# A written order for the interleaved steps of two hybrid blocks, in place of a greedy planner

## What is computed

```
out_a = sliding_window_attention(rope(norm(aq)), rope(norm(ak)), av, sinks)      # 8 heads, window 128
out_b = rmsnorm(hgrn2(bq, log_f(bf), bv)) * silu(bg)                             # 4 heads, decayed linear attention
out_c = rmsnorm(gated_delta(silu(conv4(cqkv)), beta, g)) * silu(cg)              # 4 heads, a triangular inverse per chunk
```

## Time and profile before

| what | value |
| --- | --- |
| runs | 4287.96, 4295.01, 4295.93 us; median 4295.01 |
| profiled execution, its span from the first to the last instruction | 4287.7 us (its own time outside the span is not shown) |
| PE / PE weight load / DVE / ACT / POOL busy | 93 / 76 / 60 / 38 / 3 % |
| instructions on PE / DVE / ACT | 20700 / 4066 / 2881 |
| mean granted TensorE clock | 0.955 of 2.4 GHz |
| the chain that ended last | PE 80 %, DVE 12 %, ACT 5 % |

### The profile page before, as it was taken

One profiled execution on the slowest core, in us unless ns is written; L12 is line 12 of the kernel. 1 busy time (PEld: TensorE's weight loads), 2 busy tenths in 40 slices (PEclk: granted clock), 3 DMA queues, 4 the chain that ended last, 5 costly groups with the idle time before them and its releaser, 6 DMA issues.

```text
span 4287.7 us, 51835 instructions
## 1 busy us (share of the span) xinstructions
PE 3992.2 (93%) x20700; PEld 3250.2 (76%) x20700; DVE 2571.8 (60%) x4066; ACT 1621.0 (38%) x2881; POOL 108.0 (3%) x199
## 2 busy tenths in 40 slices
PE   5879999998889999999999999999899999999988
PEld 5759778877768788887777677767777777777776
DVE  6767365654576432456667743776566667546765
ACT  3343232243443332333444243553334343334532
POOL 0000000000000000000000000000000000000000
PEclk9979799998899799989999999999899999999999
DMA  6502155532111232333232223233232322221233
GB/s 219 171 5 89 50 168 196 188 118 65 60 40 69 72 101 84 106 100 104 91 99 72 74 89 94 64 104 126 80 119 85 108 70 84 84 88 56 84 113 113
DMA packets 216641, 417.93 MB, mean 97 GB/s; under 512 B 16384, under 2 KB 61472, under 8 KB 214608
## 3 DMA queue, kind: packets, MB, share of 16 engines
q1 hardware_dynamic: 197584, 335.12, 24.4%
q0 software_dynamic: 18816, 79.49, 5.4%
HBM read 378.89 MB, written 35.67 MB: 97 GB/s over the span
## 4 chain that ended last, share of the span: by engine, by line
PE 80%; DVE 12%; ACT 5%; issue 2%; DMA 1%; SPq 0%; DVEq 0%; ACTq 0%; POOLq 0%
PE ps L632 59%; PE ps L104 13%; DVE arena L126 3%; PE ps L115 3%; ACT arena L200 3%; DVE arena L141 2%; DVE spl L126 2%; PE ps L2292 2%; DVE X L126 1%; DVE HF L126 1%; DVE sm L147 1%; PE ps L2287 1%; ACT sph L200 1%; PE ps L882 1%; PE ps L110 1%
## 5 line engine op out<-in xcount | busy, mean ns | idle before, releaser
L126 DVE TENSOR_TENSOR spl<-ring,sph 128x1024 fp32r<-128x1024 f32 (+2 forms) x556 | 651.5, 1178 | 731.9 <-ACT sph L200 730.7
L200 ACT ACTIVATE sph<-ring 128x1024 fp32r<-128x1024 f32 (+2 forms) x556 | 562.4, 1023 | 776.6 <-PE ps L632 758.3
L632 PE MATMUL ps<-sph,HTh 128*128 128x512 f32 (+3 forms) x1680 | 668.9, 398 | 22.6 <-DVE HTl L126 11.7
L632 PE MATMUL ps<-spl,HTh 128*128 128x512 f32 (+3 forms) x1680 | 621.5, 370 | 0.0
L632 PE MATMUL ps<-sph,HTl 128*128 128x512 f32 (+3 forms) x1680 | 620.6, 369 | 0.0
L200 ACT ACTIVATE arena<-ps 128x512 f32<-128x512 f32 (+2 forms) x570 | 314.0, 563 | 727.8 <-PE ps L632 484.3
L632 PE MATMUL ps<-HTh,sph 128*128 128x512 f32 x1360 | 540.5, 397 | 17.1 <-DVE spl L126 14.9
L632 PE MATMUL ps<-HTl,sph 128*128 128x512 f32 x1360 | 532.5, 392 | 0.0
L632 PE MATMUL ps<-HTh,spl 128*128 128x512 f32 x1360 | 532.1, 391 | 0.0
L104 PE MATMUL ps<-arena 128*128 128x128 f32 (+6 forms) x2264 | 374.0, 349 | 52.3 <-ACT arena L200 29.9
L632 PE MATMUL ps<-sph 128*128 128x512 f32 x992 | 405.6, 409 | 7.4 <-DVE spl L126 7.4
(11 more groups left out here) (219 smaller groups left out, 5105.3 us busy)
## 6 DMA issues: line engine op xcount, KB each, us to landing
ring<-in_w_in SPq DMA_DIRECT2D x264, 512.0 KB, 3.6
arena<-in_ada_w SPq DMA_DIRECT2D x88, 512.0 KB, 4.7
ring<-in_w_down SPq DMA_DIRECT2D x44, 512.0 KB, 3.3
ring<-in_w_gate SPq DMA_DIRECT2D x40, 512.0 KB, 3.8
ring<-in_w_up SPq DMA_DIRECT2D x40, 512.0 KB, 3.8
ring<-in_w_mem SPq DMA_DIRECT2D x32, 512.0 KB, 3.3
ring<-in_w_out SPq DMA_DIRECT2D x32, 512.0 KB, 3.9
ring<-in_w_br_ssd SPq DMA_DIRECT2D x32, 512.0 KB, 3.9
```

What stands on the lines that cost most here:

```text
L126: self.e.tensor_tensor(o, a, b, op).then_inc(*self.done.up())
L200: self.e.activation(o, a, f, **kw).then_inc(*self.done.up())
L632: ins = pe.e.matmul(o, l, r, start=k0 == 0 and i == 0 and not b.pairs, stop=k0 + b.ks == b.kt and i == 3 * b.ks - 1 and (c0 > 0 or not b.p ...
```

## The change

The planner, its constants, the lists of start slots and gates and `slot_after` are gone. For the stages `ada0`, `mix 0`, `mix 1`, `proj 0` and `proj 1` the order is written down as a string: one letter per step, `M` for main, a number before a letter repeats it. `steps_of` reads it; all engines follow it. The two `ffn` stages have main alone. The number of steps of each stream is the same as before, the generators and their waits are not touched, and SP's list of weight loads does not depend on the order. `ada0`'s string is the order that the planner made; the other four differ from the planner's throughout.

```diff
-SLACK = 1.5
-STEPS = 3
...
+STREAMS = {
+    "mix": dict(M="main", c="conv", g="gdn", a="att", h="hgrn", i="inv", m="mem", b="back", t="angles"),
+    "proj": dict(M="main", c="conv0", d="conv1", s="ssd", p="pass", g="gated", t="turns", f="diff", n="dnorm", x="cross0", y="cross1", z="cross_t", m="mgt", r="rest"),
...
+SCORES = {
...
+    ("mix", 0):
+        "14Mt2Mt2Mt6Mt4MtM2a9M2a4Mh7Mch2MaMc8MaMh8Ma4MaMac2Ma3Ma3Ma2Mc3MacMat3MaMh2MhM2c5Ma2c6gagaghaha2gagha"
+        "g2agagag2agagagag3agag3a4gimh2imhim4MiM2ihiMh2MiMihiMh2MiMhMiMiMhiMh2Mi2M3ihiMhihi2h3MiMh2MihMih2ihi"
+        "hih3i2M2h5M2iM2i3M2i25Mb",
+    ("mix", 1):
+        "26M2a3MaMa3MahMhMcMcMaMc2aMaM2aMaMcMac2Ma6M2aMhMa7Mahc6Mc2MaMacMac2h6M2gh5gah2gaga2ga2gag2a2g2ag2aga"
+        "g2agaga2gagihmimimh3MihMi3MihMiMih2MiMhiMiMhiMiMhMihi2MiMhMihiMihiM2ih2MhMiMhM2ihihMihiMh3ihi2M2hi4M"
+        "iMi3M3i10Mb15M",
+    ("proj", 0):
+        "35McMdMd3Md8Md3M2d2Md2Mc4McMdc2Mcdc7M5c2M2dMcMsMcd2Mc5MscMdM2dMcdMdMc3Md6M2cMsdc2MdsMc4Mc2dcd2Mc2M2c"
...
+        "2Mpsp2Msp2sp2sMpMpMs2pMpsM2p2Mp2M2p2MpM2pM3p2MpM3pg2M3pMp2M2pMg3MpM2p2M3pMpM3p2M2p2Mp2Mpg3pM3p19Mg4M"
+        "g6MgMg3Mgt3Mt5Mt3M2t2Mt2Mt2Mtgt8Mt2Mt3MtM4tMt4M2t5M2t2M2t15Mt7MtMt5Mt7Mt10MtM2t15M2tg3MfM2f2Mf2Mf4Mf"
...
+        "2n3MyMy6Mx3Mz3MzM2z6Mz24MmMm15Mm3M2m27M",
+    ("proj", 1):
+        "17Ms3MrMr2M2r7Msd6Md7MdMc6Mc3MdcMcMc2McMdcd2McMd5Md2MdM2cd3M2cd6Md3MdMcd2M2dcMcdMd2c5Md2McMc3Mc2d2sM"
...
+def steps_of(phase):
+    names, n = STREAMS[phase[0]], ""
+    for ch in SCORES[phase]:
+        if ch.isdigit():
+            n += ch
+            continue
+        for _ in range(int(n or 1)):
+            yield names[ch]
+        n = ""
...
-        def weave(q, phase, main, sides, gates=(), chain=(), turn=1 << 30):
+        def weave(q, phase, main, sides=()):
+
+            gens = dict(sides)
             gens["main"] = main
+            if phase in SCORES:
+                for name in steps_of(phase):
                     next(gens[name], None)
...
-            starts = [("conv", (), {0: conv[1], **conv}), ("gdn", ("conv",), slot_after(name, ("hvb", l, 1))),
-                      ("att", (), slot_after(name, ("kvb", l))),
-                      ("hgrn", (), {0: slot_after(name, ("hzb", l, 1)), 8: ("att", 99), 22: slot_after(name, ("hvb", l, 1))}),
...
-            return {slot_after(k, ("hvb", l, 1)): [("mem", 99)], w: [("hgrn", 99)], w + 8: [("inv", 99)]}
...
-            weave(q, k, main(q, k), second_sides(q, l) + [("rest", rest, (), 0)] * l, second_gates(l))
+            weave(q, k, main(q, k), second_sides(q, l) + [("rest", rest)] * l)
```

More of the change, by code:

```diff
@@ L386, in take @@
             return banks[i]
-        def weave(q, phase, main, sides, gates=(), chain=(), turn=1 << 30):
-            gens = {name: gen for name, gen, _, _ in sides}
+        def weave(q, phase, main, sides=()):
+            gens = dict(sides)
             gens["main"] = main
-            if phase in plans:
-                for name in plans[phase]:
+            if phase in SCORES:
+                for name in steps_of(phase):
                     next(gens[name], None)
[L398 to L456, removed]
-                for name, n in gates.get(slot, ()):
-                    while name not in over and count.get(name, 0) < n:
-                        go_on()
-                step("main")
-                slot += 1
-                for _ in range(STEPS):
-                    who = pick([(d, n) for d, n in can() if d <= q.t + SLACK])
-                    if who is None:
-                        break
-                    step(who)
-            slot = 1 << 30
-            while len(over) < len(gens):
-                go_on()
-            plans[phase] = plan
@@ L472, in program @@
+            for name, gen in gens.items():
+                for _ in gen:
+                    assert name == "main" and phase not in SCORES, (phase, name, q.name)
         groups, order, then, turned = {}, [], {}, {}
@@ L1876, in mixers @@
                      act=(conv1_act, gdn_act, att_act, hgrn_act, inv_act, mem_act, idle))
[L1877 to L1883 removed]
+            names = ("conv", "gdn", "att", "hgrn", "inv", "mem", "back")
             fs = f.get(q.name, [idle] * 7 if q.name == "sp" else [idle] * 5 + [mem_pool, back_pool])
[L1885 removed]
+            out = [(n, g(q, l)) for n, g in zip(names, fs)]
             if l == 0:
                 g = dict(pe=angles_pe, dve=angles_dve, act=angles_act).get(q.name, idle)
[L1888 removed]
+                out.append(("angles", g(q, l)))
             return out
@@ L2023, in first @@
                 ht_begin(q, k, xn, [(k, "xn", m) for m in (0, 1, 2, "half", 3)])
-            weave(q, k, main(q, k), mixers(q, l), mix_gates(l), CHAIN, slot_after(k, ("hvb", l, 1)))
+            weave(q, k, main(q, k), mixers(q, l))
             k = ("ffn", l)
@@ L2039, in first @@
                     layer_in(q, 0)
-            weave(q, k, main(q, k), [])
+            weave(q, k, main(q, k))
         XS = ar(0, 4, 4, 512)
@@ L2929, in second_sides @@
-            ssd[unit(12)] = [("conv0", 99), ("conv1", 99)]
-            half = pass_steps(16)
-            passes = {0: [("conv0", 99), ("conv1", 99), ("ssd", unit(18))], half: ("ssd", unit(34))}
-            gated = {0: s("z", l, 0), 2: s("z", l, 1), 4: s("z", l, 2), 6: s("z", l, 3)}
-            turns = {2 * n: s(("dq", "dk")[n // 4 % 2], l, n // 8) - 3 + n % 4 for n in range(16)}
-            turns[0] = [turns[0], ("gated", 8)]
-            b1 = slot_after(k, (("br", l, 0), 1))
-            empty = iter(())
```

89 lines of the change are left out of this document (28 added, 61 removed).

## The result

The kernel with the written order takes 4099.68 us (median of 4 runs, 4095.03 to 4101.13), the kernel before 4295.03 us (4287.96 to 4295.93). The ratio is 0.9552, 95 % interval 0.9538 to 0.9566: 4.5 % faster. The forecast was 4217 us in a range from 4155 to 4285; the sign and most of the places were right, the size was not: 195 us were saved where 78 were expected.

What follows compares the result with a forecast made beforehand. PE, busy 93 % of the span, was taken as the bound, losing time to waits and half clock in stages with side steps. Terms -25 - 12 - 6 - 50 + 15 = -78 from 4287.7, plus 7.3, gave 4217 us; range 4155 to 4285.

Steps and rivals of the forecast that it cites:

- lead-in: Mixers, between last projection slot and `gdn`: most of the dry stretch goes, moved PE work paid beside main; 25 us saved.
- `gdn` to first memory slot: Mixers: `hgrn` steps enter in layer 0, three `inv` steps leave in layer 1 and are paid after; 0 net.
- chain over the states: Mixers, after the first memory slot: main slots kept for the chain reduce half clock; 6 us saved per layer, 12.
- `hgrn`'s first step: `mix 1`: placed one slot later, so the next chunk's splits come before ACT is taken; 6 us of a 12.85 us wait saved.
- second block: `proj 0` and `proj 1`: half of 91 us of PE waits go, 46, and 4 for the end parts' clock; 50 us saved.
- new waits: Clusters of side steps and more side work beside the mixers' projection stand in front of splits; 15 us added.
- the slower rival: Clusters of side steps on DVE stand in front of splits PE needs, making them late; 4320 us, chance 0.08.
- More is saved: State chains keep full clock and second-block waits nearly all go; -140 us, 4155 us, chance 0.22.
- The clock oscillates: In the second block a finer weave would make PE's clock fall over a third of 2400 us; 4310 us, chance 0.04.

Runs made afterwards that it cites:

- head_new: Written order to the last projection slot in the mixers and to slot 208 in the second block, then the planner's order of the kernel before: 4205.5 us.
- to_memory: Written order to the first memory slot in the mixers and to slot 464 in the second block, then the planner's order of the kernel before: 4153.4 us.
- hgrn_later: The written-order kernel with the first two `hgrn` steps of `mix 1` three main slots later: 4105.34 us.

## Why the prediction was right or wrong

The terms of the sum, each with what the trace after shows:

| term | forecast | measured |
|---|---|---|
| lead-in, net of the work moved | -25 | -48.8 |
| `gdn` to first memory slot | 0 | -31.0 |
| after it (chain over the states) | -12 | -11.1 |
| `hgrn`'s first step | -6 | -2.4, within the first term |
| second block, waits and clock | -50 | -99.0 |
| new waits | +15 | none |

*Lead-in.* The place was right, and nearly all of it went: 26.7 of 27.6 us and all of the 18.5. The failed step is "PE's share of what moves must be paid beside main at full clock", 16.8 us in both layers. I took PE as full from the one window just ahead of the dry stretch. Over the whole projection it was busy 151.11 of 173 and 148.15 of 172 us: 22 and 24 idle us, of which the waits at the start of the stage (5.8) and behind `hgrn` (12.85) could take nothing, but the rest could. After the change it is busy 153.17 and 155.97, and the two projections together are 3.4 us shorter, not 16.8 longer; in `head_new` they are 2.5 shorter. Nor did all of it move there: the projections hold 19 and 45 matmuls more, where the lead-ins had 67 and 59. The others now stand in `gdn`'s stretch, which had idle time too (20 of 96.5 us). The upper bound in the text, 42 saved, named the case of work that costs nothing; the measured 48.8 (2.4 of it from `hgrn`'s wait) is beyond even that.

*`gdn`.* "0 net" failed in both layers, -7.8 and -23.2 us. The step was "three `inv` steps leave it in layer 1 and are paid after it, where PE is the bound". They took 10.8 us with them (84.0 in `to_memory` to 73.2) and were paid with nothing that shows: the part behind has 72 matmuls more and is 9.8 us shorter. In layer 0 two `inv` steps leave as well, which I had overlooked, with 8.7 us (97.3 to 88.6); and the steps that enter there, three of `hgrn` and two of `att` and not two of `hgrn`, cost about nothing (96.4 to 97.3). The other 12.4 us of layer 1 (96.4 to 84.0) went mostly with three `att` steps that now stand beside the projection (`head_new`, where little else is changed in this stretch, has 87.2).

*The chain over the states.* That the term matches (-11.1 for -12) is luck in its parts: -1.3 and -9.8 where I took 6 each. The clock of the last 50 us rose in both layers, 0.57 to 0.69 and 0.53 to 0.72. By the prediction's formula that is 45 to 32 and 48 to 29 us at half clock, and half of the difference, 6 and 10 us, to win. In layer 0 this was not won for the stage: over the whole part behind the first memory slot the clock is 0.89 in both kernels and PE was busy at half clock for 46.7 us before and 47.0 after, so the time at half clock only moved to an earlier place. In layer 1 it fell from 63.3 to 40.2 us, of which half is 11.6 us, about what the part gained.

*`hgrn`.* 12.85 became 10.47, not 7. The step failed that put the wait down to the next chunk's splits: behind the step there is always something that PE will want, here an eviction. `hgrn_later` shows it from the other side.

*Second block.* "I take half" of the waits failed; 49.5 us a stage went. The idle time fell by 74 us in the two stages, near the bound of 80 (of it 73 are in the lists of waits). The rest was never in those lists: 12.6 us at half clock, where 4 were taken, and 12 of PE's busy time, the tails at the stops for the most part, which no term had. So the bound of 80 was none: the part reached 99.

*New waits.* +15 by "the nearest rows", but they did not come: waits for `spl` fell from 27.3 to 5.1. The clusters, on which the slower rival hung, held no split late by more than 1.3 us, though they are longer than the "up to five in a row" of the prediction: the string of `proj 0` has nine side steps in a row before slot 191 and ten before slot 532. The likely reason is the one given for it, that PE has split chunks in hand; no run tests it. A cluster becomes dear when no main slot is left beside it, as the 44 us above show.

*Rivals.* "More is saved" was right in kind, at -140 still short of -190. "The clock oscillates" did not come: both stages of the second block have 0.99 where they had 0.98. The rule of the Trainium skill that the prediction weighed there ("TensorE: Matmul & The Clock Gate", "A second HAM failure mode: psum-queue depth-cycling") speaks of frequent small gaps between groups of matmuls. The trace agrees with it as far as it goes: the gaps went (42 and 44 waits to ten and nine a stage) and the clock rose. What was wrong was the step from a finer weave to more gaps.

What misled is one habit: where a term lay between two bounds I took the middle or below, and I charged moved work to PE in every stage, so that the terms were wrong on the same side together. The largest of the misses is the second block (49 us), then `gdn` (31), the lead-in (24) and the new waits (15).

## What to carry to other kernels

When side work is woven into an engine that is the bound, its loss is idle time, half clock and the tails at its stops; count all three in each stage, and look for idle time over the whole stage before you charge moved work to it. A late step costs little while main slots are left to stand beside it; when they ran out it cost about 1.2 us for a step of `conv` or `ssd` and about 4 us for one of `inv`. So the order must spread what is owed over what is left; the two planners here that delayed by a fixed slack did not. When you compare two orders by stretches, count the steps or matmuls in each stretch first: a stretch can be shorter because work has left it. And this order does not come apart into "when" and "which": with its places alone a sixth of the gain was left.

## What the runs showed of the hardware

- PE's idle time misses part of what dense work saves: in the second block the same matmuls took 14.4 and 10.4 us less busy time (1156.45 to 1142.04, 1153.46 to 1143.02), of which at most 8.9 and 3.7 are the granted clock (41.1 to 23.3 and 33.5 to 26.2 us busy at half clock).
- The granted clock in a stretch with short dependent groups rose from 0.53 to 0.72 when more main slots were put into the stretch, at almost the same busy share (49.53 of 51 and 50.06 of 51, with 184 and 246 matmuls): a PE that the profile shows as busy for 97 % of a stretch did not have the full clock there. A higher clock in one stretch was not a gain for the stage by itself: in layer 0 it rose from 0.57 to 0.69 in the last 50 us and stayed at 0.89 over the 223 us that hold them.
- `hgrn`'s first step of layer 1 keeps ScalarE for 18 us in each of the three kernels looked at (before, after, `hgrn_later`), four table loads of 1.28 us and 6.7 us of waits for VectorE among them, and everything behind it waits, the eviction of an accumulator too.
